# Layer 0's second RMS norm: eight places for the squares, weights split during the output projection, modulation tiles behind the norm

## The reference

```python
mod = silu(c) @ ada_w[l] + ada_b[l]          # six rows of 1024: shift, scale, gate, twice
h = rms_norm(x, norm1_g[l]) * (1 + sc1) + sh1
x = x + gt1 * (concat(attention(h), rwkv(h)) @ w_out[l])
h = rms_norm(x, norm2_g[l]) * (1 + sc2) + sh2
x = x + gt2 * channel_mixer(h)               # layer 0: dense SwiGLU, layer 1: top 2 of 8 experts
```

## Time and profile before

| | |
|---|---|
| median of three runs | 2429.19 us |
| the three runs | 2427.87, 2429.19, 2435.5 us |
| span of the profiled execution | 2423.8 us |
| median of the runs less that span | 5.4 us |
| TensorE busy | 2267.6 us, 94% of the span |
| VectorE, ScalarE, GpSimd busy | 1597.2, 1288.0, 166.8 us |
| mean granted TensorE clock | 0.972 of full |

### The profile page before, as it was taken

One profiled execution on the slowest core, in us unless ns is written; L12 is line 12 of the kernel. 1 busy time (PEld: TensorE's weight loads), 2 busy tenths in 40 slices (PEclk: granted clock), 3 DMA queues, 4 the chain that ended last, 5 costly groups with the idle time before them and its releaser, 6 DMA issues.

```text
span 2423.8 us, 43316 instructions
## 1 busy us (share of the span) xinstructions
PE 2267.6 (94%) x17511; PEld 1716.7 (71%) x17511; DVE 1597.2 (66%) x1887; ACT 1288.0 (53%) x1556; POOL 166.8 (7%) x162
## 2 busy tenths in 40 slices
PE   5999878898999999999788999999999999999997
PEld 3445467745888886556677678888888888888886
DVE  3474556524333332675464389898989898989897
ACT  3342456503222233433576267777777777777775
POOL 0000044300000000000353000000000000000000
PEclk9999989999999999999799989999999999999998
DMA  7222610142323226221000869999999999999997
GB/s 293 69 87 70 242 39 4 52 193 89 104 87 105 89 83 234 70 88 52 2 21 8 326 231 365 350 360 350 367 351 366 342 366 346 365 351 367 344 367 262
DMA packets 234852, 500.43 MB, mean 206 GB/s; under 512 B 9446, under 2 KB 78332, under 8 KB 227676
## 3 DMA queue, kind: packets, MB, share of 16 engines
q1 hardware_dynamic: 232544, 484.24, 55.7%
q10 hardware_dynamic: 2172, 14.20, 1.5%
HBM read 492.12 MB, written 6.29 MB: 206 GB/s over the span
## 4 chain that ended last, share of the span: by engine, by line
PE 88%; DVE 4%; ACT 3%; issue 2%; DMA 1%; POOL 1%; ACTq 0%; DVEq 0%; POOLq 0%
PE ps L612 18%; PE ps L613 18%; PE ps L614 18%; PE ps L701 11%; PE ps L605 8%; PE ps L898 6%; PE ps L640 2%; PE ps L1258 1%; PE ps L1047 1%; ACT tail L1607 1%; PE ps L1224 1%; PE ps L933 1%; POOL tail L2478 1%; PE ps L1099 1%; PE ps L1209 1%
## 5 line engine op out<-in xcount | busy, mean ns | idle before, releaser
L2378 DVE TENSOR_TENSOR weight_parts<-front,weight_parts 128x2048 fp32r<-128x2048 f32 x336 | 768.0, 2290 | 85.4 <-ACT weight_parts L1735 81.4
L1735 ACT ACTIVATE weight_parts<-front 128x2048 fp32r<-128x2048 f32 x336 | 643.6, 1919 | 248.3 <-PE ps L614 248.3
L612 PE MATMUL ps<-weight_parts,token_parts 128*128 128x512 f32 x1344 | 534.5, 398 | 1.7 <-issue 1.7
L613 PE MATMUL ps<-weight_parts,token_parts 128*128 128x512 f32 x1344 | 525.3, 391 | 0.0
L614 PE MATMUL ps<-weight_parts,token_parts 128*128 128x512 f32 x1344 | 525.0, 391 | 0.0
L612 PEld LDWEIGHTS ps<-weight_parts,token_parts 128*128 128x128 f32 x1344 | 253.1, 188 | 55.8 <-DVE weight_parts L2378 4.5
L614 PEld LDWEIGHTS ps<-weight_parts,token_parts 128*128 128x128 f32 x1344 | 253.0, 188 | 55.0
L613 PEld LDWEIGHTS ps<-weight_parts,token_parts 128*128 128x128 f32 x1344 | 253.4, 189 | 48.9
L701 PE MATMUL ps<-front,tail 128*128 128x512 f32 (+3 forms) x704 | 280.5, 554 | 6.5 <-ACT front L1427 4.4
L701 PEld LDWEIGHTS ps<-front,tail 128*128 128x128 f32 (+1 forms) x704 | 131.8, 190 | 146.1 <-issue 137.5
L898 PE MATMUL ps<-tail 64*64 64x64 f32 (+1 forms) x6976 | 169.7, 235 | 56.6 <-issue 15.3
(11 more groups left out here) (283 smaller groups left out, 2445.9 us busy)
## 6 DMA issues: line engine op xcount, KB each, us to landing
front<-in_exp_w SPq DMA_DIRECT2D x345, 1024.0 KB, 6.9
tail<-in_ffn_w SPq DMA_DIRECT2D x30, 1024.0 KB, 5.1
tail<-in_ada_w SPq DMA_DIRECT2D x27, 1024.0 KB, 8.6
tail<-in_w_in SPq DMA_DIRECT2D x24, 1024.0 KB, 5.1
front<-in_ada_w SPq DMA_DIRECT2D x21, 1024.0 KB, 10.9
tail<-in_w_out SPq DMA_DIRECT2D x8, 1024.0 KB, 6.1
parked_x<-front ACTq DMA_DIRECT2D x2, 2048.0 KB, 10.9
front<-parked_x ACTq DMA_DIRECT2D x2, 2048.0 KB, 8.5
```

Of the source, the lines that this page charges most:

```text
L612: mm(view, a_hi, b_hi, start=start, stop=False)
L613: mm(view, a_lo, b_hi, start=False, stop=False)
L1735: f_(whi[k % PARTS], at(A_RING2 + (k % RING2) * SLOT2, SLOT2), ACT.Copy).then_inc(cnt["act"].sem, 1)
L2378: ins = v.tensor_tensor(wlo[k % PARTS], at(A_RING2 + (k % RING2) * SLOT2, SLOT2), whi[k % PARTS], ALU.subtract)
```

## The change

All norms get eight places for squares, so a square waits for its source alone. For the norms over latent tokens alone the places are the context columns of `hT`. The root and reciprocal get a place of their own, `rnorm`. In norm (0, 1) the splits of the first two weight tiles move up into the output projection: the copies stand behind squares 5 and 6, the subtractions behind VectorE's additions 5 and 6. The third copy moves behind the shifts and the third subtraction behind the low parts of `h`. Modulation tiles 4 to 7 of third 3 move behind the spread, and its turn behind the first weight tile of the network. These modulation tiles lie in the memory of `h_hi` and `h_lo`, so GpSimd and VectorE get waits for their readers.

```diff
-        sqm = at(A_HTOK, 4, LAT)
-        rsm = at(A_HTOK + 1024, 2, LAT)
-
-        def rnorm_of(tag):
-            return (sqf[:, 4] if tag in ((0, 0), (0, 1), (1, 0)) else rsm[:, 0])[:, 0:P]
+        sqm = hT[:, :, 0:CTX]
+        rnorm = at(A_HTOK + 1024, P)
...
                 for c in range(DC):
-                    if tag in ((0, 1), (1, 1)) and c >= 4:
-                        ada_tile(3 + 2 * tag[0], c)
+                    if tag == (1, 1) and c >= 4:
+                        ada_tile(5, c)
                     pe.wait_ge(ev("norm_sq"), DC * norm_no[tag] + c + 1)
...
-                    if c < DC - 1:
-                        ins.then_inc(ev("norm_used"), 1)
...
-                elif tag in ((0, 1), (1, 1)):
-                    ada_turn(3 + 2 * tag[0])
+                elif tag == (0, 1):
+                    for k in range(4, DC):
+                        ada_tile(3, k)
+                elif tag == (1, 1):
+                    ada_turn(5)
...
                         banks.fill(ins, (nm, 2 * j + q))
+                    if t == 0:
+                        ada_turn(3)
...
                     source(act, c)
-                    if c >= 4:
-                        act.wait_ge(ev("norm_used"), (DC - 1) * no + c - 3)
-                    f_(sqv[:, c % 4, 0:w], xT[:, c, c0:NTOK], ACT.Square).then_inc(ev("norm_sq"), 1)
-                    if tag == (0, 1) and c >= DC - 1 - PARTS and c < DC - 1:
-                        ffn_high(c - (DC - 1 - PARTS))
+                    f_(sqv[:, c, 0:w], xT[:, c, c0:NTOK], ACT.Square).then_inc(ev("norm_sq"), 1)
+                    if tag == (0, 1) and c in (5, 6):
+                        ffn_high(c - 5)
...
                     ins.then_inc(ev("h_ready"), 1)
+                if tag == (0, 1):
+                    ada_row(3)
+                    ffn_high(2)
...
                 w = NTOK - c0
-                if tag == (0, 1):
-                    for t in range(PARTS):
-                        ffn_low(t)
                 banks.released(dve, ("norm", tag))
...
+                def early_low(c):
+                    if l == 0 and c in (5, 6):
+                        ffn_low(c - 5)
+
+                add_gated(lambda c: ("wo", l, c), l, 16, early_low)
...
                 for c in range(DC):
                     dve.wait_ge(ev("h_hi"), c + 1)
+                    if c == 0:
+                        dve.wait_ge(ev("ada_used"), (DC - 1) * 3 + 7)
+                    elif c == 4:
+                        banks.see(dve, ("ada", 3))
                     v.tensor_tensor(h_lo[:, c, :], hT[:, c, :], h_hi[:, c, :], ALU.subtract
                                     ).then_inc(ev("h_lo"), 1)
-                modulation(3)
+                ffn_low(2)
...
                     ffn_low(2 * j + 3)
+                    if j == 0:
+                        modulation(3)
...
                     pool.wait_ge(ev("h_ready"), DC * norm_no[0, 1] + c + 1)
+                    if c % 4 == 0:
+                        pool.wait_ge(ev("ada_used"), (DC - 1) * 3 + 5 + c // 4)
```

More of the change, by code:

```diff
@@ L680, in norm @@
                     ins = mm(bank[:, t * P:(t + 1) * P], ident[0:32 * n_t, 32 * t:32 * t + 1].broadcast_to([32 * n_t, P]),
-                             rnorm_of(tag)[0:32 * n_t, :], start=(t == 0), stop=True, skip_group_check=True)
+                             rnorm[0:32 * n_t, :], start=(t == 0), stop=True, skip_group_check=True)
                 banks.fill(ins, ("spread", tag))
@@ L1399, in ffn_high, with norm @@
                 f_(whi[t % PARTS][:, 0:src.shape[-1]], src, ACT.Copy).then_inc(ev("ffn_hi"), 1)
-            def norm(tag, c0, sqv, srtv, source):
+            def norm(tag, c0, sqv, source):
                 no = norm_no[tag]
@@ L1405, in norm @@
                     source(act, c)
-                    if c >= 4:
-                        act.wait_ge(ev("norm_used"), (DC - 1) * no + c - 3)
-                    f_(sqv[:, c % 4, 0:w], xT[:, c, c0:NTOK], ACT.Square).then_inc(ev("norm_sq"), 1)
-                    if tag == (0, 1) and c >= DC - 1 - PARTS and c < DC - 1:
-                        ffn_high(c - (DC - 1 - PARTS))
+                    f_(sqv[:, c, 0:w], xT[:, c, c0:NTOK], ACT.Square).then_inc(ev("norm_sq"), 1)
+                    if tag == (0, 1) and c in (5, 6):
+                        ffn_high(c - 5)
                 bank = banks.see(act, ("norm", tag))
                 r = slice(0, w // 4)
-                banks.done(f_(rnorm_of(tag)[r, :], bank[r, 0:P], ACT.Sqrt, bias=epsc[NORM_EPS][r, :], scale=1.0 / D),
+                banks.done(f_(rnorm[r, :], bank[r, 0:P], ACT.Sqrt, bias=epsc[NORM_EPS][r, :], scale=1.0 / D),
                            ("norm", tag))
-                if tag in ((0, 0), (0, 1), (1, 1)):
-                    ada_row({(0, 0): 0, (0, 1): 3, (1, 1): 5}[tag])
+                if tag in ((0, 0), (1, 1)):
+                    ada_row({(0, 0): 0, (1, 1): 5}[tag])
                 if tag[0] == 2:
@@ L1758, in _ @@
             for l in range(DEPTH):
-                seq += [lambda l=l: norm((l, 0), 0, sqf, sqf[:, 4], x_source(l, 0)), lambda l=l: project(l),
+                seq += [lambda l=l: norm((l, 0), 0, sqf, x_source(l, 0)), lambda l=l: project(l),
                         lambda l=l: attention(l), lambda l=l: chunks(l),
@@ L1762, in _ @@
                 if l == 0:
[L1763 removed]
+                    seq += [lambda: norm((0, 1), 0, sqf, x_source(0, 1)), feed_forward]
                 else:
[L1765 to L1766 removed]
+                    seq += [lambda: norm((1, 1), CTX, sqm, x_source(1, 1)), route, experts]
+            seq += [lambda: norm((2, 0), CTX, sqm, x_source(2, 0)), lambda: None]
             for f in seq:
@@ L1846, in ffn_low, with norm @@
                                 ).then_inc(ev("ffn_lo"), 1)
-            def norm(tag, c0, srtv, rstv):
+            def norm(tag, c0):
                 w = NTOK - c0
-                if tag == (0, 1):
-                    for t in range(PARTS):
-                        ffn_low(t)
                 banks.released(dve, ("norm", tag))
-                v.reciprocal(rnorm_of(tag)[0:w // 4, :], rnorm_of(tag)[0:w // 4, :]).then_inc(ev("norm_inv"), 1)
+                v.reciprocal(rnorm[0:w // 4, :], rnorm[0:w // 4, :]).then_inc(ev("norm_inv"), 1)
                 if tag in ((0, 0), (1, 1)):
@@ L2235, in first_low, with add_gated @@
                                 ).then_inc(ev("first_lo"), 1)
-            def add_gated(keys, l, g):
+            def add_gated(keys, l, g, after=lambda c: None):
                 for c in range(DC):
@@ L2437, in _ @@
             for l in range(DEPTH):
-                seq += [lambda l=l: norm((l, 0), 0, sqf[:, 4], sqf[:, 5]), lambda l=l: project(l), lambda l=l: attention(l),
+                seq += [lambda l=l: norm((l, 0), 0), lambda l=l: project(l), lambda l=l: attention(l),
                         lambda l=l: chunks(l), lambda l=l: finish(l),
@@ L2441, in _ @@
                 if l == 0:
-                    seq += [lambda: norm((0, 1), 0, sqf[:, 4], sqf[:, 5]), feed_forward]
+                    seq += [lambda: norm((0, 1), 0), feed_forward]
                 else:
-                    seq += [lambda: norm((1, 1), CTX, rsm[:, 0], rsm[:, 1]), route, experts]
-            seq += [lambda: norm((2, 0), CTX, rsm[:, 0], rsm[:, 1]), final]
+                    seq += [lambda: norm((1, 1), CTX), route, experts]
+            seq += [lambda: norm((2, 0), CTX), final]
             for f in seq:
```

7 lines of the change are left out of this document (2 added, 5 removed).

## The result

The changed kernel takes 2413.88 us (median of 5 runs, 2409.81 to 2418.38) against 2429.19 for the kernel before on the same chip (5 runs): a ratio of 0.9942, 95% interval 0.9925 to 0.9959. That is 10 to 18 us less, about 14. The profiled execution took 2413.88 us with a span of 2411.0.

What follows compares the result with a forecast made beforehand. TensorE was taken to bound the kernel, so only its waits around five RMS norms could give time: 8.4 - 0.5 + 0 + 0.3 + 0.6 = 8.8 us off 2429.19, giving 2420.4, range 2416.5 to 2426.

Steps and rivals of the forecast that it cites:

- Layer 0's second norm: From sums of squares to scaling: scaling starts at 562.45 instead of 570.81, gain 8.4 us, or 7.5 at half clock.
- Copies and subtractions: Weight splits moved into the output projection or behind shifts and low parts: they fit idle time or slack, cost nothing.
- Modulation tiles: Tiles 4 to 7 behind layer 0's second norm's spread: TensorE would idle there anyway, first cast due 1.9 us after scaling; no cost.
- The turn: Four modulation transposes moved from idle time to between two network weight tiles: 0.5 us lost, bounds 0.3 and 1.1.
- The clock at the first tile: Network's first weight tile: half clock again after about 3.3 us of idle, same 2.1 us cost; change zero, bounds +1.9 and -1.1.
- The other norms: Squares no longer held: 0.3 us gained in the first norm, 0.6 in the last, nothing in layer 1's two.
- The step that failed: Network's weight stage behind layer 0's second norm: it runs at TensorE's pace, so a start earlier by 8 us stays.
- The median: Whole program: the runs' median lies 5.4 us above the profiled span, kept for after, so 2429.19 - 8.8 = 2420.4.
- A: Half clock over the spread and a longer spell at the first tile: gain 6.8 us, time 2422.4, up to 2424; chance 0.18.
- B: GpSimd casts and VectorE low parts collide and stretch, up to 3.4 us lost: time 2420.4 to 2423.8; chance 0.06.
- C: Something unseen in the network's first tiles gives the earlier start back, no net effect: 2427 to 2431 us; chance 0.05.
- D: Second weight tile lands late, delaying addition 7 ahead of the norm: slower, 2436.5 us from a landing at 561.7; chance 0.03.

Runs made afterwards that it cites:

- the kernel with four products more: Changed kernel plus four idle, overwritten products (0.9 us) ahead of the network's eleventh weight tile; 2423.90 and 2422.44 us, 0.9976 and 0.9975 of the kernel before.

## Why the prediction was too small

- **Layer 0's second norm, 8.4.** Right: 8.2 in the start of the network, with the spread at 1.16 as taken. Forecast scaling 4.53 behind the first sum, measured 4.60.
- **Copies and subtractions, 0.** Right: neither the addition nor the last square is late, and the second copy starts right behind its square, so its tile had landed. Putting them back moves the network's start by 6.9.
- **Modulation tiles, 0.** Right: the first cast comes 1.88 behind the scaling's start, before 1.9. Its row names a modulation tile as releaser, but it comes no later than before, so the tiles hold nothing up.
- **The turn, 0.5.** 0.35 measured.
- **The clock at the first tile, 0.** Right as a change: 13.34 - 0.35 = 12.99 against 13.07; in another profile, with 13.96, it is 0.5 worse. That the modulation tiles nearer to the first tile would keep the clock, and the sum be 1.9 better, did not come true: 3.88 us of idle lie between, and the windows fall to 0.50. With the idle filled they stay at 1.00. What the Trainium skill ("TensorE: Matmul & The Clock Gate", "What's actually happening") says, that the slow clock is the default and activity releases it, agrees with both; it was the conclusion drawn from it that failed.
- **The other norms, 0.9.** 0.7 in the last norm's rows and 0.3 in the first's (from the sums' end to the root's start 0.07 in place of 0.34); in the time nothing that can be told from zero.
- **The step that failed** is "The network's weight stage behind it runs at TensorE's pace, so a start earlier by 8 stays". For the network's stage itself that held: 362.20 us before and 362.65 after, the turn included.

```profile
578.15:940.35 362.20, 361.61 (x1584) 0.99 0.30 99
564.79:927.44 362.65, 362.06 (x1588) 1.00 0.31 101
```

  What failed is that the sum ends there and puts the rest of the program at no change: TensorE's pace is not one number in it. The changed kernel runs at a mean clock of 0.974 against 0.970, worth 6 us at 1.49 per 0.001, of which some 4.5 lie outside the norm. I took the clock as a matter of the ten steps behind the idle time, put zero on it, and bounds of +1.9 and -1.1. The runs showed more than twice the larger bound, in time that the edits don't touch. The range had no term for it.
- **The median, "5.4 above that span, and I keep that"**, mixed two things. In most runs 1.8 to 2.2 us lie around a span, in some about 3. The rest was that the profiled execution of before, at clock 0.972, was a quicker one than the median run. It did no harm to the difference. The three runs on record, 2427.87 to 2435.5, already scattered by almost the forecast gain; no term of the sum followed from that.
- **Rivals.** A took the clock as a loss, right next to the norm: the spread stayed at full clock, and its 2 us did not come; the clock mattered with the other sign. B: two low parts and two casts were again stretched, no more than before:

```profile
L2521 POOL CAST token_parts<-front x8: 612/616/998, 559.3 to 565.2; 128x512 fp32r<-128x512 f32 x8
L2261 DVE TENSOR_TENSOR token_parts<-front,token_parts x8: 678/680/1099, 563.9 to 569.0; 128x512 fp32r<-128x512 f32 x8
```

  The first low part began 0.21 behind the scaling, at 563.95, as the sixth cast ended (563.32 + 0.62), and this cost no more than the 0.07 in the way from scaling to network. By the Trainium skill ("SBUF — State Buffer", "SBUF: two separate sides") one of the two would wait for the other's whole instruction, which would give a start up to 0.6 later. The start was not late by that much. Behind it the recorded times overlap and are longer (0.68 to 1.10, 0.61 to 1.00), and whether a wait of the one for the other is inside them, these rows do not say. C and D did not happen.

**Still open.** Which places make the difference between before and changed in the median run: at the second place before had its clock between the two others, and its two profiles differ by 6.7 us over the stretch. That the clock of the changed kernel is higher is shown by its 18 runs against those of before; in which places it is higher is shown, in single profiles, only against the kernel with four products more. Why the spells of half clock fall elsewhere after a shift, and what of the time follows from them, is argued from the clock of the runs and not shown: with four products more, 2 to 3 us of the loss stand neither in the work nor in the mean clock. Whether another shift of before would find the same 6 us was tried with two sizes of work only; the clock gave nothing with the one and 2.1 us with the other.

## What to carry over

In a kernel like this one, which TensorE bounds and which has waits of a few us all through it, a start earlier by 8 us behind one wait can move the time by more or less than 8, as the half-clock spells behind it fall elsewhere; here 5 us came on top of 9, and the clock accounts for most of them. So put a term of that size into the range of any small local gain, and compare kernels by many runs together with the mean granted clock of each, which parts a gain of the edit from a gain of the clock. A gain of 0.2% that stands in the clock alone belongs to this program's timing, and the next edit can lose it, as four idle products and a filled gap did.

## What was unexpected of the hardware

- TensorE work of 0.9 us, added ahead of the eleventh weight tile, lengthened the program by some 8 to 9 us, in two sets of runs; 3.4 us of it by 3.6 (ratios 0.9958 and 0.9943). At two places in the unchanged stretch the clock was the same in all profiles of one kernel (changed three, four products more two, before two), and another at one or both places in the next.
- 0.001 of mean granted clock goes with 1.49 us, over 260 runs. Were TensorE never waiting, it would be 2.4 (0.001 of 2411).
- Behind 3.88 us of idle TensorE began the first weight tile at full clock in two of the changed kernel's three profiles and fell to half about 1.5 us later; in the third it began at half. The tile's length was 13.34 and 13.31, and 13.96.
- Filling that idle time kept the clock full there, was worth 1.4 to 2.0 us on the spot, and the program as a whole lost 9.
